# Hybrid streaming encoder layer: filler groups of 7, 8 and 6 per attention step, a twelfth Strassen pair, and the convolution ahead of the values copy

## The chip, the cores and the metric

The kernel runs on one core of one Trainium2 chip. The metric is the device time of one execution in microseconds (us), as the median of several runs. Before the change it is 1660.65 us (three runs, 1660.37 to 1661.24). Profiles come from one further execution each.

## The reference

One layer, 1024 prompt tokens and 8 x 16 sample tokens, 1152 tokens in all, width 1024, float32.

```
xn = rmsnorm(x)
[h | B | C | q | k | v | g_conv | g_attn] = xn @ w_in
u  = C * h
y_c = B * causal_conv3(u)                      # 3 taps, depthwise
y_a = sliding_window_attention(q, k, v, sinks) # 16 heads, 4 kv heads, window 128, chunks of 64
x = x + (sigmoid(g_conv) * y_c + sigmoid(g_attn) * y_a) @ w_out
x = x + (silu(rmsnorm(x) @ w_gate) * (rmsnorm(x) @ w_up)) @ w_down
```

It also returns the last rows of the convolution input and the new keys and values.

## The kernel before

**Precision.** Each large product is made of three matmuls in the fast float32 format: weights and activations are split into a high part (ACT copies it out) and a low part (POOL subtracts), and high x high, high x low and low x high are added up in PSUM.

**Stages, in order of time.** Norm and transposes; values, keys and queries; an attention stage; the late pairs; the output projection; the feed-forward part in two passes. The change touches the attention stage, the late pairs and what lies between them.

**Tiles.** The columns of w_in for h, C, B, g_conv and g_attn (kinds 0 to 4) fall into four blocks i of 256 columns, each of two halves jj of 128. A tile (i, jj, kind) is one half: 128 columns against 1152 tokens. It has three parts g of 384 tokens, each of 8 groups (one per 128 rows of the contraction), each group three matmuls of 384 columns (L2209). So a tile is 24 groups or 72 matmuls. `TILES` lists the tiles made this way: all five kinds of block 0, and kinds 0 to 3 of block 1, 18 tiles.

**Late pairs.** `LATE` lists the other (i, kind), 11 of them: both halves at once, as a product of 2 x 2 blocks by Strassen's scheme with 7 block products (L2269) of 24 matmuls with 288 columns. DVE adds and subtracts blocks of weights for it (`late_weight_sums`), ACT makes the high parts, POOL the low parts, and the sums of activations t1 to t4 are prepared by POOL (`t1_part`, `t2_part`), DVE (`t_op`, `t_low`) and ACT during and behind the attention stage.

**Attention.** There are 16 steps (block of heads i, 128 queries t) of three units u: two of four heads, and one of the sample tokens. Unit z = 24 i + 3 t + u, from 0 to 47. A unit goes through
- TensorE `s1`, its scores (L2141 to L2163);
- DVE `softmax_bias`: the maxima (L1442) and two small biases (L1444, L1447);
- ACT `exps`: exponentials (L1037, L1040);
- DVE `denominator` (L1454, L1457), then ACT's scaling (L1044);
- TensorE `s2`: transposes of the probabilities (L2174);
- DVE `out_transposed`: the values copy (L1430), which takes them out of PSUM;
- TensorE `s3`: probabilities times values (L2192, L2197), then ACT `out_attention`.

TensorE's queue is written out by hand so that fillers, the groups of `TILES` in order, hide these steps: in the stretch of unit z come `s1(z)`, `MIDDLE` = 4 fillers, `s2(z - 1)` (and in every third unit `s0`, a transpose of cached keys for the next step, whose result DVE copies out in `after_s0`, L1422), 4 more fillers, `s3(z - 1)`. `PER_SLOT` is 8, so a part of a tile is just one such stretch, and its last group is the last filler. Of 432 groups 384 lie in the stretches; the last two tiles follow behind them.

DVE's queue in the stretch of unit z: `softmax_bias(z)`, `out_transposed(z - 1)`, `after_s0` if u is 2, `denominator(z)`, then for parts that ended in z - 1 the convolution `conv` (kind 1; L1485 multiplies, L1487 twice multiplies and adds) or a gate (kinds 3 and 4), then for parts that end in z the product that takes them out of PSUM (kinds 1 and 2). `units_of(z)` gives the parts that end in z, `end_slot` where a part ends.

POOL's queue in a step: the low parts of a weight slab (`split_lo_quarters`, L665, four pieces), when the tile two before has ended, placed ahead of the staging if that is the step's first stretch and behind it otherwise; the staging of the next step's queries, keys and values (`stage`: L738, L742, L748, L754, L760, L769); in block 1 part sums for t1. In the last step the part sums for t2 (L820, L822) stand there. SP loads slabs and late weights, ACT splits high parts and evacuates kinds 0, 3 and 4.

Behind the stretches DVE's order is again by hand: a convolution, `t_op`, `t_low`, the products of the last two tiles and `late_weight_sums(0)`. The last tile's second and third parts swap banks (`LAST_BANKS`), and the first late product waits for the bank of the second part (`bank_free[2]`), the second product for the other two.

Of the kernel before, what the change touches and what calls it, by code (L numbers as in the profile page):

```python
# [28 lines left out]
ALU = mybir.AluOpType  # L29
# [34 lines left out]
        [(1, jj, kind) for jj in range(2) for kind in range(4)]  # L64
# [8 lines left out]
PER_SLOT = 8  # L73
MIDDLE = 4


def end_slot(n, g):

    return (24 * n + 8 * g + 7) // PER_SLOT
# [12 lines left out]
INSIDE = 2 * SLOTS * PER_SLOT // 24  # L92
# [106 lines left out]
class Slab:  # L199


    def __init__(self, first, per=0, i=0):
        self.n = first + per * i
        self.slot = first % 2
        self.turn = first // 2 + (per // 2) * i
        self.split = self.slot if isinstance(first, int) and first < OUT_SLAB else 1 - self.slot


LATE = [(1, 4)] + [(i, kind) for i in (2, 3) for kind in range(5)]
# [25 lines left out]
def build(nc, io):  # L235
    ctx = ExitStack()
    with ctx:
# [247 lines left out]
        def late_view(n, part):  # L485
            return ring_l[:, (n + 1) % LRING, part, :].rearrange("p (k c) -> p k c", k=4)
# [423 lines left out]
        def _(act):  # L910
# [185 lines left out]
            def late_slot_hi(n):  # L1096

                v, prod = n // 7, LATE_ORDER[n % 7]
                if n >= LRING:
                    act.wait_ge(l_used, n - LRING + 1)  # L1100
                else:
                    act.wait_ge(gemm_ready, 3 * (LATE_FEAT - 1 + (n + 1) % LRING // 2))
# [9 lines left out]
            unit(16, 0)  # L1112
            act.wait_ge(small_out, 32)
            act.activation(t1_hi[:, :, :], t1_f[:, :, :], ACT.Copy).then_inc(t_hi, 1)
            unit(16, 1)
            unit(16, 2)
            late_slot_hi(0)
            unit(17, 0)
            unit(17, 1)
            late_slot_hi(1)  # L1120
            unit(17, 2)
# [6 lines left out]
            def late_pair(v):  # L1128
# [16 lines left out]
                if v == 0:  # L1145
                    act.wait_ge(sg_used, 18)
                else:
                    act.wait_ge(lu2_done, v)
# [201 lines left out]
        def _(dve):  # L1350
# [119 lines left out]
            def conv(i, jj, g):  # L1470
# [5 lines left out]
                for k in range(3):  # L1476
# [12 lines left out]
                if g == 2:  # L1489
# [73 lines left out]
            for i in range(2):  # L1563
                for t in range(STEPS):
                    for u in range(3):
# [6 lines left out]
                        else:  # L1572
                            bi, bz = divmod(z - 1, SLOTS)
# [6 lines left out]
                        for n, g in units_of(z - 1):  # L1580
                            if TILES[n][2] == 1:
                                conv(*TILES[n][0:2], g)
                            if TILES[n][2] >= 3:
                                unit(n, g)
# [4 lines left out]
            conv(1, 1, 2)  # L1589
            dve.wait_ge(t_part, T2_PARTS)  # L1590
            dve.wait_ge(s3_done, 2 * SLOTS)
            t_op(t4_f[:, :, :], x_quad(0, 1, 0).bitcast(F32), t2_f[:, :, :], ALU.subtract)
            t_op(t3_f[:, :, :], t2_f[:, :, :], x_quad(0, 0, 0).bitcast(F32), ALU.subtract)
            t_low(1, t2_lo[:, :, :], t2_f[:, :, :], t2_hi[:, :, :])
            unit(16, 0)
            unit(16, 1)
# [3 lines left out]
            unit(16, 2)  # L1600
# [3 lines left out]
            unit(17, 0)  # L1604
            t_op(t4_f[:, :, :], t4_f[:, :, :], x_quad(1, 1, 0).bitcast(F32), ALU.add)
            unit(17, 1)
            unit(17, 2)
# [32 lines left out]
            def late_pair(v):  # L1640
# [39 lines left out]
                if kind == 3:  # L1680
# [4 lines left out]
                if v == 0:  # L1685
                    dve.wait_ge(sg_used, 18)
# [328 lines left out]
        def _(pe):  # L2015
# [200 lines left out]
            for i in range(2):  # L2216
                for t in range(STEPS):
                    for u in range(3):
# [22 lines left out]
            for k, group in enumerate(groups[2 * SLOTS * PER_SLOT:]):  # L2241
# [82 lines left out]
            def row_units(slot, s, act_slot):  # L2324
                for t in range(NT):
# [7 lines left out]
                    row_unit(3 + t % DU, ws[1 - slot], act_slot, t)  # L2333
# [28 lines left out]
            for n, (c, hf, t) in enumerate(LAST_ROWS):  # L2362
# [6 lines left out]
                row_unit(4 + n % 4, third if c == 2 else ws[1 - hf], c % 2, t)  # L2369
# [142 lines left out]
```

## Time and profile before

| what | us |
|---|---|
| median of 3 runs | 1660.65 (1660.37 to 1661.24) |
| the profiled execution | 1661.15 |
| its span | 1659.3 |
| TensorE busy | 1641.2 (99%) |
| DVE busy | 1041.4 (63%) |
| POOL busy | 972.5 (59%) |
| ACT busy | 726.4 (44%) |

The span runs from the first to the last instruction of the profiled execution; its own time is 1.85 us longer. Matmuls are pipelined, so a matmul's shown duration is longer than the distance from its start to the next one's, and a busy TensorE is one with no gap, not one at its peak. An idle time in brackets behind a row is that of its engine just ahead of the row, with what ended it; "issue" means that the profile names no releaser.

### The profile page before, as it was taken

The numbers are of one execution on the slowest core, as the hardware profiler recorded it, in microseconds if no ns is written. First come the engines' busy times: TensorE is split into PE (matmuls) and PEld (weight loads), VectorE is DVE, ScalarE is ACT, GpSimd is POOL, SyncE is SP. The second block draws the span as 40 slices with busy tenths as digits, with TensorE's granted clock in tenths as the row PEclk, the third lists the DMA queues.
The fourth block names the chain that finished last, engine by engine and source line by source line (L and its number), as shares of the span: only waits on it lengthen the run. The fifth ranks groups of instructions, "written<-read, shape, count | busy, mean of one in ns | idle before, by whom it ended". The sixth has DMA issues, their size and how long they took to land.

```text
span 1659.3 us, 28301 instructions
## 1 busy us (share of the span) xinstructions
PE 1641.2 (99%) x10775; PEld 1535.3 (93%) x10775; DVE 1041.4 (63%) x1602; ACT 726.4 (44%) x1635; POOL 972.5 (59%) x873
## 2 busy tenths in 40 slices
PE   7999999999999999999999999999999999999999
PEld 7999889998899999999889899999989999999998
DVE  6466664655659664475676767667687555555555
ACT  6333566666664313223155544544444433333331
POOL 3544533445554544443359978878878666666662
PEclk9999999999999999999999999999999999999999
DMA  5211111111110111114121333333233222222222
GB/s 180 49 39 38 48 33 33 33 33 33 41 38 13 52 52 52 52 45 159 53 90 51 105 113 95 98 113 102 91 130 104 84 77 89 77 80 86 87 79 76
DMA packets 124834, 120.44 MB, mean 73 GB/s; under 512 B 24218, under 2 KB 106430, under 8 KB 124704
## 3 DMA queue, kind: packets, MB, share of 16 engines
q1 hardware_dynamic: 119136, 115.89, 22.3%
q10 hardware_dynamic: 4896, 2.36, 0.5%
q8 instruction: 84, 1.38, 0.3%
q0 software_dynamic: 672, 0.43, 0.1%
q14 instruction: 46, 0.38, 0.1%
HBM read 113.34 MB, written 5.32 MB: 72 GB/s over the span
## 4 chain that ended last, share of the span: by engine, by line
PE 64%; DVE 2%; POOL 1%; issue 0%; ACT 0%; DVEq 0%; ACTq 0%
PE banks L2381 29%; PE banks L2442 15%; PE banks L2269 14%; PE banks L2319 5%; PE banks L2209 1%; PE banks L2464 1%; POOL ring_a L863 1%; PE banks L2358 0%; DVE act L1613 0%; DVE w_sums L1804 0%; DVE O L1659 0%; POOL ring_o L863 0%; DVE gate L1939 0%; DVE xc_full L1826 0%; POOL w_lo L658 0%
## 5 line engine op out<-in xcount | busy, mean ns | idle before, releaser
L2381 PE MATMUL banks<-xc_hi,ring_a 128*128 128x256 f32 (+1 forms) x1200 | 248.2, 296 | 0.6 <-POOL ring_a L863 0.6
L863 POOL TENSOR_TENSOR ring_a<-raw_f,ring_a 128x512 fp32r<-128x512 f32 x133 | 191.2, 1450 | 19.4 <-ACT ring_a L1232 18.4
L2381 PEld LDWEIGHTS banks<-xc_hi,ring_a 128*128 128x128 f32 x1200 | 196.6, 190 | 1.4 <-issue 1.0
L2381 PE MATMUL banks<-xc_lo,ring_a 128*128 128x256 f32 (+1 forms) x600 | 177.7, 296 | 0.0
L2209 PE MATMUL banks<-x_hi,w_hi 128*128 128x384 f32 x432 | 154.0, 356 | 0.3 <-DVE branch L1519 0.3
L1964 DVE TENSOR_TENSOR X<-banks,X 128x512 f32<-128x512 f32 x190 | 123.2, 683 | 36.4 <-PE banks L2442 36.2
L2209 PE MATMUL banks<-x_hi,w_lo 128*128 128x384 f32 x432 | 145.2, 336 | 0.0
L2209 PE MATMUL banks<-x_lo,w_hi 128*128 128x384 f32 x432 | 145.1, 336 | 0.0
L2269 PE MATMUL banks<-x_hi,late_ring 128*128 128x288 f32 x704 | 143.6, 295 | 0.0
L665 POOL TENSOR_TENSOR w_lo<-w_raw,w_hi 128x256 fp32r<-128x256 f32 x72 | 52.1, 756 | 147.2 <-ACT w_hi L916 147.2
L2381 PE MATMUL banks<-xc_hi,ring_o 128*128 128x256 f32 (+1 forms) x640 | 134.7, 296 | 0.0
L2442 PE MATMUL banks<-ring_a,h_act 128*128 128x512 f32 x570 | 133.3, 391 | 1.0 <-DVE X L1964 0.6
L2442 PEld LDWEIGHTS banks<-ring_a,h_act 128*128 128x128 f32 x570 | 105.9, 188 | 24.7 <-DVE X L1964 2.3
L863 POOL TENSOR_TENSOR ring_a<-w_sums,ring_a 128x512 fp32r<-128x512 f32 x60 | 85.2, 1420 | 73.8 <-ACT ring_a L1232 73.8
L2381 PEld LDWEIGHTS banks<-xc_lo,ring_a 128*128 128x128 f32 x600 | 113.8, 190 | 0.4
L2269 PEld LDWEIGHTS banks<-x_hi,late_ring 128*128 128x128 f32 x704 | 113.9, 188 | 0.0
L1232 ACT ACTIVATE ring_a<-raw_f 128x512 fp32r<-128x512 f32 x133 | 81.3, 624 | 73.3 <-PE banks L2442 54.3
L2269 PE MATMUL banks<-t_hi,late_ring 128*128 128x288 f32 x528 | 108.5, 295 | 0.0
L1393 DVE RECIPROCAL branch<-branch 128x384 f32<-128x384 f32 x30 | 76.6, 2552 | 48.5 <-ACT branch L986 48.5
L2381 PEld LDWEIGHTS banks<-xc_hi,ring_o 128*128 128x128 f32 x640 | 105.7, 190 | 0.2
L2269 PE MATMUL banks<-x_lo,late_ring 128*128 128x288 f32 x352 | 103.6, 294 | 0.0
L848 POOL TENSOR_TENSOR late_ring<-late_raw,late_ring 128x512 fp32r<-128x512 f32 x44 | 66.9, 1526 | 60.5 <-ACT late_ring L1107 60.5
(330 smaller groups left out, 4610.2 us busy)
## 6 DMA issues: line engine op xcount, KB each, us to landing
raw_f<-in_w_gate SPq DMA_DIRECT2D x88, 256.0 KB, 3.0
raw_f<-in_w_up SPq DMA_DIRECT2D x88, 256.0 KB, 3.1
raw_f<-in_w_down SPq DMA_DIRECT2D x88, 256.0 KB, 2.8
w_raw<-in_w_in SPq DMA_DIRECT2D x60, 256.0 KB, 3.4
late_raw<-in_w_in SPq DMA_DIRECT2D x44, 256.0 KB, 3.0
X<-in_x_prompt SPq DMA_DIRECT2D x16, 512.0 KB, 7.3
w_raw<-in_w_out SPq DMA_DIRECT2D x16, 256.0 KB, 3.0
out_y_prompt<-X SPq DMA_DIRECT2D x16, 256.0 KB, 2.0
```

What stands on the lines that cost most here:

```text
L665: ins = gp.tensor_tensor(ws[slab.split][1][:, part], raw[slab.slot][:, part], ws[slab.split][0][:, part].bitcast(F32), ALU.subtract)
L848: gp.tensor_tensor(late_view(n, 1), late_source(prod), late_view(n, 0).bitcast(F32), ALU.subtract)\
L863: gp.tensor_tensor(slot_view(n, 1), slot_source(n), slot_view(n, 0).bitcast(F32), ALU.subtract).then_inc(f_lo, 1)
L1232: act.activation(slot_view(n, 0), slot_source(n), ACT.Copy).then_inc(f_hi, 1)
L1393: dve.reciprocal(kr[:, bank[0], :], kr[:, bank[0], :]).then_inc(h_rs, 1)
L1964: dve.tensor_tensor(x, banks[:, row_bank(n), :], x, ALU.add).then_inc(y_free, 1)
L2209: mm = pe.matmul(banks[:, bank, 0:G], ws[n % 2][w][:, kt * P:(kt + 1) * P], xs[x][:, kt, g * G:(g + 1) * G], start=(kt == 0 and z == 0), s ...
L2269: mm = pe.matmul(banks[:, 2 * BANK_OF_PROD[prod] + u, 0:LN], late_view(n, w)[:, k, :], late_x(prod, x, u, k), start=(starts and k == 0 and ...
L2319: mm = pe.matmul(banks[:, bank, :], acts[act_slot][:, k, x, t * P:(t + 1) * P], split[w][:, k * 512:(k + 1) * 512], start=(k == 0 and n == ...
L2381: mm = pe.matmul(banks[:, bank, 0:nb], ring(n)[:, w, k * P:(k + 1) * P], xc[x][:, X_OF_PROD[j], k, 0:nb], start=(start and k == 0 and z == 0),
L2442: mm = pe.matmul(banks[:, row_bank(n), :], rows, ring(SLOT0[r] + 2 * hf + k)[:, w, :], start=(k == 0 and o == 0), stop=(k == 1 and o == 2))
L2464: mm = pe.matmul(banks[:, row_bank(n), :], rows, ring(SLOT0[r] + 2 * hf + k)[:, w, :], start=(c == NCH - 2 and k == 0 and o == 0), stop=(c ...
```

## The change

Two tiles, kind 3 of block 1, leave `TILES` (16 tiles left) and (1, 3) joins `LATE` (12 pairs). The fillers in the stretches are no longer 8 each but 7, 8 and 6 for the three units of a step, with 4, 5 and 3 of them ahead of `s2`. A part of a tile now ends anywhere in a stretch. DVE runs the convolution between `softmax_bias` and `out_transposed`, save for the third tap of a tile's last part, which stays behind `denominator`. Behind the stretches DVE's list is ordered anew; it has all three convolutions of tile (1, 1, 1). The late ring's slots are numbered so that the first two lie where the last tile but one had its weights. The first late pair's waits are those of a pair of kind 3.

```
-        [(1, jj, kind) for jj in range(2) for kind in range(4)]
+        [(1, jj, kind) for jj in range(2) for kind in range(3)]
...
-PER_SLOT = 8
-MIDDLE = 4
+GROUPS = (7, 8, 6)
+AHEAD = (4, 5, 3)
+FIRST_GROUP = [sum(GROUPS) * (z // 3) + sum(GROUPS[:z % 3]) for z in range(2 * SLOTS + 1)]
 def end_slot(n, g):
-    return (24 * n + 8 * g + 7) // PER_SLOT
+    last = 24 * n + 8 * g + 7
+    return sum(last >= first for first in FIRST_GROUP) - 1
...
-LATE = [(1, 4)] + [(i, kind) for i in (2, 3) for kind in range(5)]
+LATE = [(1, 3), (1, 4)] + [(i, kind) for i in (2, 3) for kind in range(5)]
...
-            return ring_l[:, (n + 1) % LRING, part, :].rearrange("p (k c) -> p k c", k=4)
+            return ring_l[:, n % LRING, part, :].rearrange("p (k c) -> p k c", k=4)
...
@@ DVE, in the stretch of unit z
                         else:
+                            for n, g in units_of(z - 1):
+                                if TILES[n][2] == 1:
+                                    conv(*TILES[n][0:2], g, range(3) if g < 2 else range(2))
                             bi, bz = divmod(z - 1, SLOTS)
                             out_transposed(bi, *divmod(bz, 3))
...
                         for n, g in units_of(z - 1):
-                            if TILES[n][2] == 1:
-                                conv(*TILES[n][0:2], g)
+                            if TILES[n][2] == 1 and g == 2:
+                                conv(*TILES[n][0:2], g, (2,))
                             if TILES[n][2] >= 3:
                                 unit(n, g)
...
@@ DVE, behind the stretches
             out_transposed(1, STEPS - 1, 2)
-            conv(1, 1, 2)
             dve.wait_ge(t_part, T2_PARTS)
             dve.wait_ge(s3_done, 2 * SLOTS)
             t_op(t4_f[:, :, :], x_quad(0, 1, 0).bitcast(F32), t2_f[:, :, :], ALU.subtract)
+            unit(14, 0)
+            conv(1, 1, 0)
+            t_low(1, t2_lo[:, :, :], t2_f[:, :, :], t2_hi[:, :, :])
+            unit(14, 1)
+            conv(1, 1, 1)
             t_op(t3_f[:, :, :], t2_f[:, :, :], x_quad(0, 0, 0).bitcast(F32), ALU.subtract)
-            t_low(1, t2_lo[:, :, :], t2_f[:, :, :], t2_hi[:, :, :])
-            unit(16, 0)
-            unit(16, 1)
+            unit(14, 2)
             dve.wait_ge(t_step, 2)
             dve.wait_ge(t_lo, 1)
             t_low(2, t1_lo[:, :, :], t1_f[:, :, :], t1_hi[:, :, :])
-            unit(16, 2)
-            t_op(t3_f[:, :, :], t3_f[:, :, :], x_quad(1, 0, 0).bitcast(F32), ALU.subtract, 2)
+            conv(1, 1, 2)
+            unit(15, 0)
             dve.wait_ge(t_lo, 2)
             late_weight_sums(0)
-            unit(17, 0)
+            unit(15, 1)
+            t_op(t3_f[:, :, :], t3_f[:, :, :], x_quad(1, 0, 0).bitcast(F32), ALU.subtract, 2)
+            unit(15, 2)
             t_op(t4_f[:, :, :], t4_f[:, :, :], x_quad(1, 1, 0).bitcast(F32), ALU.add)
-            unit(17, 1)
-            unit(17, 2)
...
@@ TensorE, in the stretch of unit z
-                        for k, group in enumerate(groups[z * PER_SLOT:(z + 1) * PER_SLOT]):
+                        for k, group in enumerate(groups[FIRST_GROUP[z]:FIRST_GROUP[z + 1]]):
...
-                            if k == MIDDLE:
+                            if k == AHEAD[u]:
```

## Rows read from the trace of the kernel before

**Rows 1.** The page, busy time of the engines: us, share of the span, instructions.

```profile
PE 1641.2 (99%) x10775; PEld 1535.3 (93%) x10775; DVE 1041.4 (63%) x1602; ACT 726.4 (44%) x1635; POOL 972.5 (59%) x873
```

**Rows 2.** The chain that ended last: start us, us, what; its late pairs.

```profile
535.76 235.34 PE banks L2269 x1776
```

**Rows 3.** TensorE in order of time, one attention step: start, us, line, operation.

```profile
388.51 0.28 PE L2141 MATMUL banks<-mask,halves 64*128 64x256 bf16 x2
...
393.27 0.33 PE L2209 MATMUL banks<-x_hi,w_lo 128*128 128x384 f32 x1
...
393.79 0.33 PE L2209 MATMUL banks<-x_hi,w_lo 128*128 128x384 f32 x1
393.96 0.38 PE L2197 MATMUL banks<-probsT,cache_v_rows 128*128 128x128 f32 x2
...
394.50 0.28 PE L2141 MATMUL banks<-mask,halves 64*128 64x256 bf16 x2
...
400.68 1.08 PE L2192 MATMUL banks<-probsT,v_stage 128*64 128x256 f32 x8
401.69 0.23 PE L2160 MATMUL banks<-window,halves 128*128 128x128 bf16 x1
...
407.56 1.08 PE L2192 MATMUL banks<-probsT,v_stage 128*64 128x256 f32 x8
408.57 0.28 PE L2141 MATMUL banks<-mask,halves 64*128 64x256 bf16 x2
```

**Rows 4.** DVE in order of time, the same step.

```profile
392.05 0.42 DVE L1430 COPY probsT<-banks 128x256 f32<-128x256 f32 x1 [0.37 <-PE banks L2174]
...
397.02 0.16 DVE L1447 TENSOR_TENSOR soft<-soft,sinkb 128x4 f32<-128x4 f32 x1
398.69 1.23 DVE L1430 COPY probsT<-banks 128x1024 f32<-128x1024 f32 x1 [1.51 <-PE banks L2174]
...
403.11 0.16 DVE L1447 TENSOR_TENSOR soft<-soft,sinkS 128x1 f32<-128x1 f32 x1
405.44 1.23 DVE L1430 COPY probsT<-banks 128x1024 f32<-128x1024 f32 x1 [2.17 <-PE banks L2174]
406.58 0.34 DVE L1422 TENSOR_SCALAR cache_kT<-banks,qnw 128x128 f32<-128x128 f32 x1
```

**Rows 5.** TensorE in order of time, the first two units: where it waited.

```profile
192.75 0.40 PE L2144 MATMUL banks<-mask,halves 64*128 64x256 bf16 x4 [0.32 <-ACT soft L1040]
...
199.94 1.08 PE L2192 MATMUL banks<-probsT,v_stage 128*64 128x256 f32 x8 [0.82 <-issue]
```

**Rows 6.** DVE in order of time, the first unit's values copy.

```profile
198.63 1.21 DVE L1430 COPY probsT<-banks 128x1024 f32<-128x1024 f32 x1
```

**Rows 7.** DVE in order of time, convolutions alone and beside POOL.

```profile
306.62 0.40 DVE L1485 TENSOR_SCALAR branch<-u,cwT 128x384 f32<-128x384 f32 x1
...
307.06 1.27 DVE L1487 SCALAR_TENSOR_TENSOR branch<-u,cwT,branch 128x384 f32<-128x384 f32 x2
...
502.55 3.36 DVE L1487 SCALAR_TENSOR_TENSOR branch<-u,cwT,branch 128x384 f32<-128x384 f32 x2
```

**Rows 8.** POOL in order of time, the step of rows 3.

```profile
390.92 2.82 POOL L665 TENSOR_TENSOR w_lo<-w_raw,w_hi 128x256 fp32r<-128x256 f32 x4 [8.31 <-ACT w_hi L916]
...
397.11 0.73 POOL L754 TENSOR_TENSOR k_lo<-k_full,k_hi 128x256 fp32r<-128x256 f32 x1
397.80 1.43 POOL L760 TENSOR_TENSOR q_lo<-O,q_hi 128x256 fp32r<-128x256 f32 x2
```

**Rows 9.** POOL in order of time, part sums beside the convolution at 502.55.

```profile
499.51 5.99 POOL L822 TENSOR_TENSOR t_full<-t_full,x_lo 128x576 f32<-128x576 f32 x4
```

**Rows 10.** TensorE in order of time, its waits from unit 47 to the late pairs.

```profile
508.33 1.08 PE L2192 MATMUL banks<-probsT,v_stage 128*64 128x256 f32 x8 [0.57 <-issue]
...
523.04 0.41 PE L2209 MATMUL banks<-x_hi,w_hi 128*128 128x384 f32 x1 [0.30 <-DVE branch L1519]
```

**Rows 11.** Busy by window, the two last tiles: window, length, PE, PEld, DVE, ACT, POOL.

```profile
509.30:535.60 26.30, 26.00 (x153) 25.67 (x152) 25.89 (x28) 8.69 (x14) 6.67 (x5) 1.00 0.07 21
```

More of the change, by code:

```diff
@@ L89, in slab_after @@
     return [n + 2 for n in range(len(TILES) - 2) if end_slot(n, 2) + 1 == z and z <= 2 * SLOTS]
-INSIDE = 2 * SLOTS * PER_SLOT // 24
 PASSES = ((0, 0), (0, 1), (1, 0))
@@ L205, in __init__ @@
         self.turn = first // 2 + (per // 2) * i
-        self.split = self.slot if isinstance(first, int) and first < OUT_SLAB else 1 - self.slot
-LATE = [(1, 4)] + [(i, kind) for i in (2, 3) for kind in range(5)]
+        self.split = self.slot
+LATE = [(1, 3), (1, 4)] + [(i, kind) for i in (2, 3) for kind in range(5)]
 GATED = [sum(kind >= 3 for _, kind in LATE[:v]) for v in range(len(LATE))]
@@ L1101, in late_slot_hi @@
                 else:
-                    act.wait_ge(gemm_ready, 3 * (LATE_FEAT - 1 + (n + 1) % LRING // 2))
+                    act.wait_ge(gemm_ready, 3 * (LATE_FEAT - 1 + n // 2))
                 if prod in (A11_PROD, A12_PROD, A22_PROD):
@@ L1145, in late_pair @@
                 if v == 0:
-                    act.wait_ge(sg_used, 18)
+                    act.wait_ge(sg_used, 12)
                 else:
@@ L1468, in sample_cols, with conv @@
                 return a[:, SEQ:TOK].rearrange("p (b c) -> p b c", b=DEC_B)
-            def conv(i, jj, g):
+            def conv(i, jj, g, steps=range(3)):
                 lo, hi = u_parts(g)
@@ L1475, in conv @@
                 dve.wait_ge(bank_free[LAST_BANKS[g] if n == len(TILES) - 1 else g], PAIR_FEAT + n + 1)
-                for k in range(3):
+                for k in steps:
                     w = cwT[:, k, bass.ds(2 * i + jj, 1)]
@@ L1488, in conv @@
                     ins.then_inc(conv_step, 1)
-                if g == 2:
+                if g == 2 and 2 in steps:
                     j = bass.ds(2 * i + jj, 1)
@@ L1592, in _ @@
             t_op(t4_f[:, :, :], x_quad(0, 1, 0).bitcast(F32), t2_f[:, :, :], ALU.subtract)
+            unit(14, 0)
+            conv(1, 1, 0)
+            t_low(1, t2_lo[:, :, :], t2_f[:, :, :], t2_hi[:, :, :])
+            unit(14, 1)
+            conv(1, 1, 1)
             t_op(t3_f[:, :, :], t2_f[:, :, :], x_quad(0, 0, 0).bitcast(F32), ALU.subtract)
-            t_low(1, t2_lo[:, :, :], t2_f[:, :, :], t2_hi[:, :, :])
-            unit(16, 0)
-            unit(16, 1)
+            unit(14, 2)
             dve.wait_ge(t_step, 2)
@@ L1599, in _ @@
             t_low(2, t1_lo[:, :, :], t1_f[:, :, :], t1_hi[:, :, :])
-            unit(16, 2)
-            t_op(t3_f[:, :, :], t3_f[:, :, :], x_quad(1, 0, 0).bitcast(F32), ALU.subtract, 2)
+            conv(1, 1, 2)
+            unit(15, 0)
             dve.wait_ge(t_lo, 2)
             late_weight_sums(0)
-            unit(17, 0)
+            unit(15, 1)
+            t_op(t3_f[:, :, :], t3_f[:, :, :], x_quad(1, 0, 0).bitcast(F32), ALU.subtract, 2)
+            unit(15, 2)
             t_op(t4_f[:, :, :], t4_f[:, :, :], x_quad(1, 1, 0).bitcast(F32), ALU.add)
-            unit(17, 1)
-            unit(17, 2)
             dve.wait_ge(gemm_ready, 3 * LATE_FEAT)
@@ L1679, in late_pair @@
                     dve.wait_ge(conv_step, 36 + 6 * (i - 2) + 3)
-                if kind == 3:
+                if v == 0:
+                    for b in range(3):
+                        dve.wait_ge(bank_free[b], LATE_FEAT)
+                elif kind == 3:
                     dve.wait_ge(lc11_done, v)
@@ L1684, in late_pair @@
                     dve.wait_ge(l_gated, g0)
-                if v == 0:
-                    dve.wait_ge(sg_used, 18)
                 dve.wait_ge(l_used, late_done(v, S3_PROD))
@@ L2240, in _ @@
                             s3(*before, used)
-            for k, group in enumerate(groups[2 * SLOTS * PER_SLOT:]):
+            for k, group in enumerate(groups[FIRST_GROUP[2 * SLOTS]:]):
                 if k == 0:
@@ L2332, in row_units @@
                         pe.wait_ge({0: lc11_done, 1: lc21_done, 3: lc12_done}[t], len(LATE))
-                    row_unit(3 + t % DU, ws[1 - slot], act_slot, t)
+                    row_unit(3 + t % DU, ws[slot], act_slot, t)
             for c in range(3):
@@ L2368, in _ @@
                 pe.wait_ge(d_free, (43, 44, 45, 45)[n] if n < 4 else LAST_BASE + n - 3)
-                row_unit(4 + n % 4, third if c == 2 else ws[1 - hf], c % 2, t)
+                row_unit(4 + n % 4, third if c == 2 else ws[hf], c % 2, t)
                 if n == 12:
```

## The prediction

> **What bounds the kernel now.** I read the busy shares first: TensorE is busy 99% of the span [rows 1]. With one engine that full, a change can only move the time by giving TensorE fewer or shorter instructions, or by making it wait. Then the chain of waits: through the Strassen products of the late pairs it is TensorE alone, 1776 matmuls in 235.34 us, so 132.5 ns each [rows 2]. Then TensorE's order of time through one attention step [rows 3]: the scores of its three units start at 388.51, 394.50 and 401.69, the next step at 408.57. A step takes 20.06 us, its units 5.99, 7.19 and 6.88, and fillers run from end to end: three filler matmuls, one group, take 0.52 us (393.27 to 393.79). I write "slot" for the stretch of one unit, slots 0 to 47, and give times in a slot from its first scores matmul.
>
> Last, what TensorE would wait for next. At the end of each slot it multiplies the previous unit's probabilities by the values (L2192, L2197), which needs DVE's values copy (L1430), in third slots also the copy of the cached keys behind it (L1422). The copy starts when the transposes end. In a second slot it runs from 398.69 for 1.23, the product starts at 400.68: 0.76 to spare. In a third slot the keys copy ends at 406.92, the product starts at 407.56: 0.64 to spare. In a first slot it is 1.49 [rows 3, 4]. TensorE can start 0.10 behind such a copy: where it waited for one, the copy ended at 199.84 and the product began at 199.94 [rows 5, 6].
>
> **The change, part by part.**
>
> **Fewer fillers.** Three groups leave each of the 16 steps: 48 groups at 0.52. The first gives nothing. In slot 0 TensorE already waits for ACT's exponentials (idle 0.32), and in slot 1 for the values copy (idle 0.82) [rows 5]; that copy follows a chain on DVE which no filler sets, so both slots end when they did. 47 x 0.52 = 24.4 us off.
>
> **One more late pair.** 7 products x 24 matmuls = 168 x 132.5 ns = 22.3 us on [rows 2]. ACT, POOL and DVE take this pair like the eleven others, beside which TensorE never waited. The weights loaded are the same bytes. Both parts together: 2.1 us off.
>
> Here a rule speaks against the change. The rows price a matmul by its columns: 173 ns at 384 columns [rows 3], 132.5 ns at 288 [rows 2], so 168 of the short cost less than 144 of the long. The Trainium skill (TensorE: Matmul & The Clock Gate, Back-to-back issue gap) gives sustained spacings of 81 ns at 128 columns and 131 ns at 512. An estimate on a line between them, 114 and 102 ns, makes the late pair 17.1 us and the two tiles 16.5, so the sum would be 3.3 us worse than mine. I go by the rows, both taken in this kernel.
>
> **The places of the three transposes and values products.** Behind the transposes (AHEAD 4, 5, 3) every slot keeps three groups where it had four. The spare times above fall by 0.52: first slots 0.97, second 0.24, third 0.12. All are over 0.10, the last by a hair. I take no cost for slots without a convolution.
>
> **The convolution ahead of the values copy.** It is a multiply (0.40) and two multiply-adds (0.63 each) on DVE, 1.7 with the gaps [rows 7]. Behind the denominators it delayed no values copy; now it can. Three tiles of products h*C lie in the slots, and their nine parts run in slots 5, 6, 7; 19, 20, 21; 39, 40, 41 (a part's convolution runs in the slot after its last group; tiles of 24 groups against steps of 21 give the slots). The last part of each tile leaves its third tap behind the denominators, so it counts four short instructions.
>
> Third slots (5, 20, 41): DVE ends the maxima and biases at 1.58 (403.11 + 0.16), the convolution at 3.28, and the values copy starts at 3.75 - 0.52 = 3.23 [rows 4]. So near that I take no cost.
>
> Second slots (7, 19, 40): biases end at 2.68, the values copy is due at 4.19 + 0.52 = 4.71 [rows 4]. Alone the convolution would end at 4.38. But POOL stages the next step's queries and keys there, from 2.61 to 4.73 [rows 8]. DVE and POOL instructions on SBUF operands don't run together: against POOL's pieces of 1.50 us each multiply-add took 1.68 instead of 0.63 [rows 7, 9]. Here the pieces are 0.72, so my estimate is 0.87 for the multiply (it waits out the piece running until 3.34) and 1.1 per multiply-add: end at 5.7, values copy until 6.9, product at 7.0 in place of 6.18: 0.8 us. Four short instructions in slot 7: 1.0. Together 2.6.
>
> First slots (6, 21, 39): biases also at about 2.7, convolution 4.4, copy of one block (0.42 to 0.43) 4.8, product due at 5.45 - 0.52 = 4.93 [rows 3, 4]. Slot 6 fits. Slot 39 meets the end of a POOL part sum which now stands behind a slab split of slot 38: 0.3, my guess. Slot 21 meets the split of a weight slab, four pieces from 2.41 to 5.23 [rows 8]; each of the four instructions waits for one, they end near 6.0, the product starts near 6.5: 1.5.
>
> Sum 4.4 us on. Below it, the cost is 0 if POOL's pieces and the convolution miss each other; above, 8.8 if each instruction waits for twice as much. I take the middle, because these POOL pieces stand at fixed distances from the scores in every step, so the overlap is not a matter of luck.
>
> **The last slots.** In slot 47 TensorE idled 0.57 [rows 10] because DVE was late from a convolution stretched by POOL's part sums. No convolution is left there, but the small bias steps still meet those sums: 0.3 off (between 0 and 0.6).
>
> **Behind the slots.** DVE was busy 25.89 of the 26.30 us of the two last tiles [rows 11], TensorE waited once for it, 0.30 [rows 10]. DVE now has three convolutions there instead of one (3.4 more) but comes in without a backlog. It must release the bank of the last tile's second part before the late products start, and by the order in the code that falls about when TensorE arrives: 0.3 on, between -0.3 and 2. Queued behind that release are the release for the second product and the sums for the fourth, with about 1 us each to spare.
>
> Sum: -24.4 + 22.3 + 4.4 - 0.3 + 0.3 = 2.3 us on. The profiled execution took 1661.15 us (span 1659.3), 0.5 over the median of 1660.65. The same 2.3 on the median is 1662.9.
>
> **The rivals.**
>
> *The convolution hides.* If POOL's pieces miss it, 4.4 falls away: -2.1, or 1658.5 us. For it: alone it fits every slot but the third ones, by 0.05. Against it: the pieces in [rows 8] lie right across it. Chance 0.25. It is a gain, but inside the 0.2% (3.3 us) that a measurement of this kernel can tell from no change. For more than that, all waits of the old slots and tail would have to vanish too: 0.04 of this.
>
> *The short slots lose their margin (slower).* Place: second and third slots without convolution, some 26 of them. With 0.24 and 0.12 left against 0.10, it decides from 0.14 and 0.02 us of delay of the values copy. A wait of 0.15 in each adds 3.9 to the forecast: 1666.8 us. For it: the 0.02. Against it: no row shows DVE late for the transposes there. Chance 0.15.
>
> *The step doesn't shrink.* If the softmax chain sets the pace, TensorE stands still where fillers were and the late pair is paid in full: 1660.65 + 22.3 = 1683. Against it: every slot had at least 0.6 to spare [rows 3, 4]. Chance 0.01.
>
> *Matmuls cost by number, not by columns.* Then the late pair costs 24 matmuls more than the tiles, 24 x 132.5 ns = 3.2 in place of -2.7, and the time is 1668.8. The rows speak plainly against it; 0.01. The rule cited above points this way, and by the two spacings the trace does not agree.
>
> **How the numbers follow.** Forecast 0.58, convolution hides 0.25, margin 0.15, the rest 0.02. The forecast's own range is 1659.5 to 1666.5 from the bounds of its terms; about a quarter of it lies over 1664.0, the limit of slower. Slower: 0.58 x 0.25 + 0.15 + 0.02 = 0.31. Faster by over 0.2%: 0.04. No change: 0.65. The range 1658.2 to 1666.6 takes in the hidden case and most of the margin case.
>
> **What would show it.** The filler line L2209 with 1152 matmuls instead of 1296, L2269's successor with 2016 instead of 1848 at 132.5 ns. A step near 18.5 us between first-unit scores. New TensorE waits before the values product in slots 7, 19, 21 and 40 of 0.7 to 1.6 us, with multiply-adds of about 1.1 us there; none in 5, 6 and 20. If these slots show no wait, the contention step is wrong; if plain second and third slots show waits, the margin step is; if the time falls by more than 3 us, something in the old slots cost what I did not see.

## The result, and the profile after

The changed kernel takes **1663.1 us** (median of 20 runs, 1662.55 to 1663.9) against 1660.65 for the kernel before: a ratio of 1.0015, 95% interval 1.0008 to 1.0022. That is slower, by less than the 0.2% counted as no change here. The profiled execution took 1663.34 us, its span is 1661.6 us, 2.3 over the span before. In the page of the changed kernel, busy us and instructions by engine, to be read against [rows 1]:

```profile
span 1661.6 us, 28376 instructions
PE 1640.2 (99%) x10799; PEld 1534.2 (92%) x10799; DVE 1044.9 (63%) x1609; ACT 729.7 (44%) x1639; POOL 985.0 (59%) x872
```

TensorE is busy 1.0 us less than before and the span is 2.3 longer: the work became a little cheaper and TensorE waits 3.3 us more. Where, the stretches tell. First the kernel before: the attention stage (first scores to the last transposes), the two tiles behind it, and its first late pair. Columns: window, length, PE, PEld, DVE, ACT, POOL, granted clock, DMA share, GB/s.

```profile
186.47:509.35 322.88, 321.17 (x2310) 288.24 (x2309) 194.14 (x404) 209.54 (x711) 147.71 (x223) 1.00 0.12 34
509.35:535.60 26.25, 25.95 (x153) 25.66 (x152) 25.84 (x28) 8.69 (x14) 6.67 (x5) 1.00 0.07 21
535.60:557.86 22.26, 22.26 (x169) 22.26 (x169) 15.64 (x15) 11.13 (x15) 14.33 (x8) 1.00 0.16 48
```

The same of the changed kernel, the last line being its first late pair:

```profile
186.43:489.37 302.94, 297.54 (x2166) 264.71 (x2165) 185.81 (x393) 206.13 (x706) 143.79 (x215) 1.00 0.11 33
489.37:515.08 25.71, 25.71 (x153) 25.70 (x151) 22.73 (x31) 8.41 (x14) 9.48 (x6) 1.00 0.08 22
515.08:537.99 22.91, 22.76 (x170) 22.33 (x169) 20.38 (x15) 10.13 (x13) 18.06 (x8) 1.00 0.15 47
```

The attention stage is 19.94 us shorter, but TensorE's idle time in it (length less PE's busy time) went from 1.71 to 5.40. The two tiles are 0.54 shorter. There is one more late pair at 22.26, and the first one takes 0.65 more than that. Sum: -19.94 - 0.54 + 22.26 + 0.65 = +2.43, the 2.3 of the spans to within 0.15. In the chain that ended last, the late pairs read as 1872 matmuls at 132.7 ns, where [rows 2] has 132.5, behind a slow first pair:

```profile
518.54 6.60 PE banks L2276 x48
525.16 248.33 PE banks L2276 x1872
```

The new idle time is in TensorE's waits of the changed kernel (total us, times, longest). L2199 and L2204 are the values products, L2192 and L2197 of before:

```profile
PE banks L2199 <- issue: 2.5, 4, 0.8
PE banks L2204 <- issue: 1.4, 2, 1.1
PE banks L2151 <- ACT soft L1041: 0.8, 1, 0.8
PE banks L2199 <- DVE cache_kT L1423: 0.4, 1, 0.4
```

Of these, 0.82 of the first row (slot 1) and 0.32 of the third (slot 0) are old [rows 5]. Slot 0 waits 0.52 more, because it has a group less and ends no sooner; that part of the 3.69 us costs nothing by itself.

"issue" hides the releaser here. It is found by laying DVE beside TensorE. TensorE in order of time from slot 19 (a second slot, scores at 305.46) to slot 21:

```profile
305.46 0.28 PE L2148 MATMUL banks<-mask,halves 64*128 64x256 bf16 x2
312.29 1.08 PE L2199 MATMUL banks<-probsT,v_stage 128*64 128x256 f32 x8 [0.58 <-issue]
...
318.14 1.08 PE L2199 MATMUL banks<-probsT,v_stage 128*64 128x256 f32 x8
319.16 0.28 PE L2148 MATMUL banks<-mask,halves 64*128 64x256 bf16 x2
325.40 0.46 PE L2204 MATMUL banks<-probsT,cache_v_rows 128*128 128x128 f32 x2 [1.15 <-issue]
```

DVE in order of time in slot 19, with the keys copy of slot 20 and the two multiplies of slot 21:

```profile
306.50 1.23 DVE L1443 TENSOR_REDUCE soft<-banks 128x4 f32<-128x1024 f32 x1 [1.05 <-PE banks L2161]
...
308.06 0.97 DVE L1486 TENSOR_SCALAR branch<-u,cwT 128x384 f32<-128x384 f32 x1
309.07 1.98 DVE L1488 SCALAR_TENSOR_TENSOR branch<-u,cwT,branch 128x384 f32<-128x384 f32 x2
310.98 1.21 DVE L1431 COPY probsT<-banks 128x1024 f32<-128x1024 f32 x1
...
317.65 0.34 DVE L1423 TENSOR_SCALAR cache_kT<-banks,qnw 128x128 f32<-128x128 f32 x1
...
322.24 1.58 DVE L1486 TENSOR_SCALAR branch<-u,cwT 128x256 f32<-128x256 f32 x2
```

POOL in order of time, beside it and beside slot 21:

```profile
306.74 0.62 POOL L749 TENSOR_TENSOR k_hi<-kT,qnw 128x256 fp32r<-128x256 f32 x1
...
308.07 0.74 POOL L755 TENSOR_TENSOR k_lo<-k_full,k_hi 128x256 fp32r<-128x256 f32 x1
308.78 1.86 POOL L761 TENSOR_TENSOR q_lo<-O,q_hi 128x256 fp32r<-128x256 f32 x2
310.58 0.73 POOL L770 COPY v_stage<-V 128x256 f32<-128x256 f32 x1
...
321.55 2.87 POOL L666 TENSOR_TENSOR w_lo<-w_raw,w_hi 128x256 fp32r<-128x256 f32 x4 [10.24 <-ACT w_hi L917]
```

The convolution takes 2.99 us where it takes 1.7 alone [rows 7], DVE goes straight on to the values copy, and the product starts 0.10 behind that copy's end, TensorE having idled 0.58. In slot 21 the product waits 1.15 in the same way, behind a convolution that meets the slab split. POOL pays too: its two pieces take 0.93 each instead of 0.72 [rows 8]. The Trainium skill (SBUF — State Buffer, Who interferes with whom) says that a DVE instruction with two SBUF inputs contends with a GpSimd instruction that reads SBUF, and that one with at most one SBUF input, outside the modes that use both ports, does not, a reduction never. The trace agrees in direction: the multiply-add goes from 0.63 to 0.99, while the maxima (1.23) and the values copy (1.21), both read from PSUM with POOL at work beside them, stay as they were alone. The multiply goes from 0.40 to 0.97 although a single tensor is its input; no row tells in which mode it ran.

Against the plain length of their kind (5.47, 7.19, 5.84 us), the slots of the changed kernel are longer by

| slot | kind | us over plain | what is late |
|---|---|---|---|
| 7, 19, 40 | second | 0.54, 0.65, 0.64 | convolution beside POOL's staging |
| 21 | first | 1.39 | convolution beside a slab split |
| 39 | first | 0.46 | convolution behind a bias stretched by a part sum |
| 29 | third | 0.48 | the two small biases beside POOL |
| 36 | first | 0.32 | the same, by way of the exponentials |
| 14 third slots | third | 0.02 to 0.04 each, 0.5 together | copy of the cached keys |
| 5, 6, 20, 41 | first, third | none (third: as above) | |
| 0 and 1 | first, second | none: 14.49 together, as before | |

### The profile page after: what moved, and what is told of

It reads as the page before. It is cut to its first block, busy times and chain, and to the rows that moved or that the text cites. A ratio compares the mean times of both kernels' runs of the same rounds, so it can differ in the third digit from the quotient of the medians.

```text
span 1661.6 us, 28376 instructions
## 1 busy us (share of the span) xinstructions
PE 1640.2 (99%) x10799; PEld 1534.2 (92%) x10799; DVE 1044.9 (63%) x1609; ACT 729.7 (44%) x1639; POOL 985.0 (59%) x872
## 3 DMA queue, kind: packets, MB, share of 16 engines
q1 hardware_dynamic: 118112, 115.89, 22.3%
q8 instruction: 84, 1.38, 0.3%
## 4 chain that ended last, share of the span: by engine, by line
PE 94%; DVE 2%; POOL 1%; issue 1%; ACT 1%; DMA 0%; SPq 0%; DVEq 0%; ACTq 0%
PE banks L2388 28%; PE banks L2276 16%; PE banks L2449 15%; PE banks L2216 12%; PE banks L2035 7%; PE banks L2326 5%; PE banks L2199 2%; PE banks L2181 2%; PE banks L2058 2%; PE banks L2161 1%; PE banks L2071 1%; PE banks L2471 1%; POOL ring_a L864 1%; PE banks L2048 0%; PE banks L2170 0%
## 5 line engine op out<-in xcount | busy, mean ns | idle before, releaser
L2276 PE MATMUL banks<-x_hi,late_ring 128*128 128x288 f32 x768 | 156.8, 295 | 0.0
L2216 PE MATMUL banks<-x_hi,w_hi 128*128 128x384 f32 x384 | 137.9, 359 | 0.0
L2216 PE MATMUL banks<-x_hi,w_lo 128*128 128x384 f32 x384 | 129.1, 336 | 0.0
L2216 PE MATMUL banks<-x_lo,w_hi 128*128 128x384 f32 x384 | 129.0, 336 | 0.0
L2276 PEld LDWEIGHTS banks<-x_hi,late_ring 128*128 128x128 f32 x768 | 124.2, 188 | 0.3 <-DVE x_lo L1546 0.3
L2276 PE MATMUL banks<-t_hi,late_ring 128*128 128x288 f32 x576 | 118.5, 295 | 0.1
L2276 PE MATMUL banks<-x_lo,late_ring 128*128 128x288 f32 x384 | 113.1, 294 | 0.0
L849 POOL TENSOR_TENSOR late_ring<-late_raw,late_ring 128x512 fp32r<-128x512 f32 x48 | 75.2, 1573 | 62.0 <-ACT late_ring L1108 62.0
L849 POOL TENSOR_TENSOR late_ring<-late_sums,late_ring 128x512 fp32r<-128x512 f32 x36 | 53.5, 1489 | 85.0 <-ACT late_ring L1108 85.0
```

Of the source, the lines that this page charges most:

```text
L849: gp.tensor_tensor(late_view(n, 1), late_source(prod), late_view(n, 0).bitcast(F32), ALU.subtract)\
L2216: mm = pe.matmul(banks[:, bank, 0:G], ws[n % 2][w][:, kt * P:(kt + 1) * P], xs[x][:, kt, g * G:(g + 1) * G], start=(kt == 0 and z == 0), s ...
L2276: mm = pe.matmul(banks[:, 2 * BANK_OF_PROD[prod] + u, 0:LN], late_view(n, w)[:, k, :], late_x(prod, x, u, k), start=(starts and k == 0 and ...
```

## The experiments

**What does the convolution cost ahead of the copy, if POOL is kept away?** The changed kernel, with POOL's staging held in the three steps whose second slot has a convolution:

```
             if q >= 1:
                 gp.wait_ge(s1_done, 3 * (q - 1) + 2)
+                if q - 1 in (2, 6, 13):
+                    gp.wait_ge(pt_ready, 3 * (q - 1) + 1)
             gp.wait_ge(k_step, q + 1)
```

> The changed kernel; in the three steps whose second slot has a convolution, POOL's low parts of keys and queries wait until the values copy of that slot is done. Theory (DVE and POOL hold each other up): the convolutions of slots 7, 19 and 40 take 1.7 us in place of 2.9, the slots fall to 7.19, 1.8 us together, less up to 0.5 for what POOL now does later: 1661.3 to 1661.9 us. Rival (the convolution is too long for its place by itself): 1662.8 to 1663.4, slots 7, 19 and 40 as before.

Measured: **1660.76 us** (1660.42 to 1661.89), 2.3 below the changed kernel; to the kernel before 0.9999, interval 0.999 to 1.0008. DVE in slot 19, in order of time:

```profile
307.67 0.41 DVE L1488 TENSOR_SCALAR branch<-u,cwT 128x384 f32<-128x384 f32 x1
308.12 1.27 DVE L1490 SCALAR_TENSOR_TENSOR branch<-u,cwT,branch 128x384 f32<-128x384 f32 x2
309.77 1.23 DVE L1433 COPY probsT<-banks 128x1024 f32<-128x1024 f32 x1 [0.39 <-PE banks L2183]
```

The convolution is back at its length alone, DVE now waits 0.39 for the transposes, and slots 7, 19 and 40 are plain (7.19). So in those slots the whole cost was the meeting with POOL, not the new place. The stage is 1.81 shorter, the sum of the three slots; the profiled execution (1661.75, the second longest of the eleven) is 1.59 below that of the changed kernel. The median fell by 0.5 more than the stage, and by more than expected, which no row settles.

**Is the new place worth anything?** All convolutions put back behind the denominators, the rest of the change kept:

```
-                            for n, g in units_of(z - 1):
-                                if TILES[n][2] == 1:
-                                    conv(*TILES[n][0:2], g, range(3) if g < 2 else range(2))
...
-                            if TILES[n][2] == 1 and g == 2:
-                                conv(*TILES[n][0:2], g, (2,))
+                            if TILES[n][2] == 1:
+                                conv(*TILES[n][0:2], g)
```

> The changed kernel with all nine convolutions back behind the denominators; fillers, late pairs and everything else as changed. Theory (the convolution ahead of the values copy makes TensorE wait): slots 7, 19, 21, 39 and 40, which are 0.54, 0.65, 1.39, 0.46 and 0.64 us longer than plain ones (3.7 together), fall back to 7.19 and 5.47 us. New delays are possible where the four-part convolutions of slots 7 and 41 now end after the next scores: up to 0.4 in slot 8 and 1.6 in slot 42. So 1659.4 to 1661.5 us. Rival (behind the denominators the convolution holds up the next maxima by as much, which is why it was moved): 1662.5 us or more.

Measured: 1663.07 us, ratio 1.0016 (1.0007 to 1.0025), the same as the changed kernel. The waits moved: slots 7, 19, 21, 39 and 40 are plain, but the slot after a convolution is long, 8 by 0.56, 22 by 0.54, 42 by 2.25, because DVE comes to its maxima 2.3, 2.7 and 3.2 us late. DVE around slot 42 (scores at 449.45):

```profile
448.47 1.30 DVE L1486 TENSOR_SCALAR branch<-u,cwT 128x256 f32<-128x256 f32 x2
449.80 3.77 DVE L1488 SCALAR_TENSOR_TENSOR branch<-u,cwT,branch 128x256 f32<-128x256 f32 x4
...
453.64 1.22 DVE L1443 TENSOR_REDUCE soft<-banks 128x4 f32<-128x1024 f32 x1
```

The estimate in the expectation was too small for slot 42. The expected 1659.4 to 1661.5 us was missed, and the rival of the expectation came true: with short slots a convolution finds no place on DVE that is free by itself, 3.35 us of waits behind, 3.68 ahead. Slot 43 added 1.41 in this profile from another cause (the last section).

**The third slots' missing 0.03.** The same kernel with the transposes a group earlier in second and third slots:

```
-AHEAD = (4, 5, 3)
+AHEAD = (4, 4, 2)
```

> As e1_conv_behind, and the transposes one group earlier in second and third slots (4, 4, 2 groups ahead in place of 4, 5, 3). Theory (the 0.03 to 0.04 us that 14 third slots are longer than counted is the keys copy ending too near the values product): third slots at 5.84 instead of 5.88, 0.5 us; the denominators come 0.5 earlier, so what e1 has of new delays in slots 8 and 42 shrinks too: 0.5 to 1.5 us below e1. Rival (those 0.04 are the cost of issuing, not a wait): within 0.2 us of e1.

Measured: 1661.7 us, 1.4 below. The plain third slots take 5.83 to 5.84 instead of 5.87 to 5.88, 0.5 in all; slot 42 is 0.77 better, slot 2 0.26 worse. There the transpose of the cached keys starts at 202.90, 0.14 behind the last of ACT's rows that take the first unit's output out of PSUM; the probabilities, which the text of a later run blames, are scaled by 201.37, ahead of their transposes at 201.73.

**How near is the edge?** The changed kernel with the transposes one group later everywhere:

```
-AHEAD = (4, 5, 3)
+AHEAD = (5, 6, 4)
```

> The changed kernel with the transposes one group later in every slot (5, 6, 4 in place of 4, 5, 3). Theory (the spare time behind the copies is 0.97, 0.24 and 0.15, and 0.10 to 0.15 of it is the least there can be): second slots without convolution get 0.38 longer (13 of them), third slots 0.5 (16), first slots don't change: 13 us, so 1676 us. Rival (there is more slack than the profile shows, as in the queue of TensorE): under 1668 us.

Measured: 1675.23 us in a single execution, 1676 expected. The waits of this kernel name the late part:

```profile
PE banks L2199 <- DVE cache_kT L1423: 7.4, 15, 0.5
PE banks L2199 <- issue: 6.5, 17, 0.8
```

Third slots are longer by 0.54 to 0.56, second by 0.38 to 0.39, first ones not at all, save slot 42 by 0.54. Call the 0.10 us from a copy's end to the product's start the hand-over. With a margin m over it, a group of 0.52 should cost 0.52 - m: that gives 0.14 for second slots (predicted 0.24 - 0.10), and for third slots 0.52 on top of the 0.03 that they had already lost (predicted 0.12 - 0.10 to spare). The margins read in the trace of before were right to 0.06.

**Slots 21, 29, 36 and 39.** The changed kernel with the slab split ahead of slot 21's step held until the values copy, and the part sums of three steps held until the biases:

```
                     for n in slab_after(z):
+                        if z == 21:
+                            gp.wait_ge(pt_ready, z)
                         split_lo_quarters(Slab(PAIR_SLAB + n))
...
+                    if i == 1 and t in (1, 3, 4):
+                        gp.wait_ge(soft_done, 5 * {1: 29, 3: 36, 4: 39}[t] + 3)
                     if i == 1 and 1 <= t < 7:
```

> The changed kernel with GpSimd's work moved out of the way of VectorE in three places and nothing else: the weight split ahead of slot 21's step waits for slot 21's values copy, and the t1 sums that fell on slots 29, 36 and 39 wait for those slots' second bias. The convolution stays ahead of the values copy. Theory (what slows the convolution and the biases is GpSimd reading and writing SBUF at the same time): slot 21 goes back to its plain 5.47 us or to within 0.1 of it (it had 1.39 more), slots 29, 36 and 39 lose 0.48, 0.32 and 0.2 to 0.45 of what they had over plain; together 2.2 to 2.7 less, 1660.4 to 1660.9 us; slots 7, 19 and 40, where nothing is held, keep their 0.5 to 0.65 each. Rival (slots 21 and 39 are long because a convolution ahead of the copy is too long for a first slot with seven fillers, whatever GpSimd does): slot 21 keeps 1.0 or more of its extra and slot 39 its 0.46, and the time stays at 1662.0 to 1662.6. Second rival (GpSimd's held work comes late and meets another slot): the four slots are cured and others get longer, 1661.5 or more.

Measured: 1663.01 us over eleven executions, one of which took 5241.14 us, with no row to explain it; the other ten have a median of 1662.8. That is a gain of 0.3 us at most where 2.2 to 2.7 were expected, and the reason is in one slot. Slots 21, 29 and 36 are plain, 2.2 us less, as the theory says. Slot 39 went from 0.46 to 1.94 over. DVE and POOL there:

```profile
433.38 0.16 DVE L1452 TENSOR_TENSOR soft<-soft,sinkb 128x4 f32<-128x4 f32 x1
433.46 0.41 DVE L1490 TENSOR_SCALAR branch<-u,cwT 128x384 f32<-128x384 f32 x1
433.91 3.34 DVE L1492 SCALAR_TENSOR_TENSOR branch<-u,cwT,branch 128x384 f32<-128x384 f32 x2
```

```profile
433.62 3.21 POOL L810 TENSOR_TENSOR t_full<-t_full,x_lo 128x576 f32<-128x576 f32 x2 [2.48 <-DVE soft L1452]
```

The second bias releases the sums, and in a slot with a convolution the convolution stands right behind that bias: each multiply-add waits out one sum of 1.6 us (1.67 in place of 0.63). The stage is 0.70 shorter (1.39 + 0.48 + 0.32 - 1.48); the span is 0.3 shorter, as the stage began 0.35 later in this profile.

**All held together:** the holds of the first experiment and of the last one, and the transposes of the third slots a group earlier (`AHEAD = (4, 5, 2)`):

> The kernel with the staging held back in three steps (1660.76 us) plus the held split and sums, plus the transposes of the probabilities one filler group earlier in the third slots (AHEAD of 2 instead of 3 there), where the key copy had been 0.03 to 0.04 late in 14 slots. Theory: 2.2 to 2.7 for the held work and 0.3 to 0.5 for the third slots, less up to 0.3 in slot 2, where the scaled probabilities come late: 1657.8 to 1658.6 us, faster than the kernel before (1660.65) by 0.13 to 0.17 per cent. Rival (cured slots only hand the delay on): 1660 or more.

Measured: 1660.26 us (1659.82 to 1662.59), over the 1658.6 expected. Slots 7, 19, 40, 21, 29, 36 and all third slots but the first are plain; slot 2 has 0.31, and slot 39 keeps its 1.96, since its sums are still released ahead of the convolution. That slot alone is as large as the miss; the three longest executions are a matter of the last section.

**Are fillers free in slots 0 and 1?** Three groups more there, and six fillers instead of seven in slots 3, 9 and 12 (the "2+1" in the text is a slip for these):

```
-FIRST_GROUP = [sum(GROUPS) * (z // 3) + sum(GROUPS[:z % 3]) for z in range(2 * SLOTS + 1)]
+FIRST_GROUP = [sum(GROUPS) * (z // 3) + sum(GROUPS[:z % 3]) + (0, 2, 3, 3, 2, 2, 2, 2, 2, 2, 1, 1, 1, 0)[min(z, 13)]
+               for z in range(2 * SLOTS + 1)]
```

> The kernel of the run before it with two more filler groups in slot 0 and one more in slot 1, taken from slots 2+1, 9 and 12 (three first slots with six fillers: slots 3, 9 and 12). Slots 0 and 1 take 6.29 and 8.20 us, 0.8 and 1.0 over what their fillers need, because a chain other than the fillers ends them. Theory (fillers there are free): slots 0 and 1 grow by 0.2 at most together, slots 3, 9 and 12 lose 0.52 each: 1.2 to 1.6 less, 1656.4 to 1657.3 us. Rival (the fillers only push the chain back, since matrix products of the chain stand behind them in the same order): slots 0 and 1 grow by 1.0 or more, and the time stays within 0.5 of the run before it. Second rival (a first slot of six fillers is too short for the values copy and the exponentials): slots 3, 9, 12 lose less than 0.3 each.

Measured: 1659.39 us (1658.71 to 1660.09). Slots 0 and 1 take 6.41 and 8.07, 14.48 together as before, so three groups (1.56 us) cost nothing there; slots 3, 9 and 12 lose 0.53 each. The time fell by only 0.87, and 1656.4 to 1657.3 us, set before the run ahead of it was known, was missed: that run had not come down to 1658.6, and in this profile slot 40 took 1.54 more (the last section).

**The sums of slot 39 behind the copy.** The sums of slot 39's step wait for the values copy, which is behind the convolution, and slot 2 keeps its three fillers ahead of the transposes:

```
-                    if i == 1 and t in (1, 3, 4):
-                        gp.wait_ge(soft_done, 5 * {1: 29, 3: 36, 4: 39}[t] + 3)
+                    if i == 1 and t in (1, 3):
+                        gp.wait_ge(soft_done, 5 * {1: 29, 3: 36}[t] + 3)
+                    if i == 1 and t == 4:
+                        gp.wait_ge(pt_ready, 39)
...
-                            if k == AHEAD[u]:
+                            if k == AHEAD[u] + (z == 2):
```

> The kernel with filler groups moved into slots 0 and 1 (1659.39 us) with two repairs: the t1 sums of slot 39's step wait for slot 39's values copy, which comes behind the convolution, and not for its second bias, which comes ahead of it (there the two sums started together with the convolution, each multiply-add took 1.67 us, and the slot got 1.94 over plain); and slot 2 keeps its three fillers ahead of the transposes. Theory (a convolution ahead of the copy costs a first slot nothing but what GpSimd's SBUF work beside it adds): slot 39 returns to 5.47 us or to within 0.1 of it, slot 2 loses 0.3, and with the 1.7-us idle time of slot 39 gone the stretch at half clock behind it (1.54 us in slot 40 of the profile of the run before) is gone from all executions: 1656.7 to 1657.5 us in median, and no execution above 1658.2. Rival (slot 39 is too long with the convolution ahead, alone too): the slot keeps 0.4 or more and the median is 1657.6 or more.

Measured: **1657.0 us** (1656.6 to 1657.88), ratio to the kernel before 0.9979, interval 0.997 to 0.9988: below the kernel before, though not clearly by more than the 0.2% counted as no change, and 6.1 us below the changed kernel. Its busy times by window, the attention stage:

```profile
186.06:482.50 296.44, 296.09 (x2166) 263.35 (x2165) 179.31 (x393) 205.86 (x706) 142.41 (x215) 1.00 0.12 34
```

TensorE idles 0.35 us in the stage, against 5.40 in the changed kernel and 1.71 before. DVE and POOL in slot 39:

```profile
429.45 0.41 DVE L1495 TENSOR_SCALAR branch<-u,cwT 128x384 f32<-128x384 f32 x1
429.89 1.27 DVE L1497 SCALAR_TENSOR_TENSOR branch<-u,cwT,branch 128x384 f32<-128x384 f32 x2
431.08 0.42 DVE L1440 COPY probsT<-banks 128x256 f32<-128x256 f32 x1
```

```profile
431.58 2.81 POOL L813 TENSOR_TENSOR t_full<-t_full,x_lo 128x576 f32<-128x576 f32 x2 [4.42 <-DVE probsT L1440]
```

With POOL away, the convolution ahead of the copy costs this first slot nothing. The one cost left is 0.16 in slot 40, where the staging, pushed back by the held sums, meets the convolution. Of the 3.65 us to the kernel before, 1.6 belong to the moved groups. They were not tried on the kernel before, whose slots 0 and 1 wait too [rows 5]; nor were the holds, but in its stage TensorE waits nowhere outside slots 0, 1 and 47 (0.32 + 0.82 + 0.57 are the whole 1.71). The other 2 or so are what the change is worth with POOL ordered around it.

## Why the prediction was right

Predicted 1662.9, measured 1663.1. The mechanism held in the main: short slots, a late pair by its columns, the convolution against POOL. That it came out to 0.2 us is luck, since the errors of its terms, -1.2 and +1.3, cancel.

| step | predicted | found | from |
|---|---|---|---|
| fewer fillers | -24.4 | -24.4 | stage -19.94, less all rows below that lie in it |
| convolution ahead of the copy | +4.4 | +3.68 | slots 7, 19, 21, 39, 40 |
| plain slots' margin | 0 | +0.5 | 14 third slots at 0.02 to 0.04 |
| small biases beside POOL | not seen | +0.80 | slots 29 and 36 |
| slot 47 | -0.3 | -0.51 | its wait, 0.57 to 0.06 |
| behind the slots | +0.3 | +0.1 | -0.54 in the two tiles, +0.65 in the first late pair |
| late pair | +22.3 | +22.26 | each of the other eleven |
| sum | +2.3 | +2.43 | spans: 2.3 |

**Fewer fillers.** The -24.4 found is what the other rows leave, but the plain slots say the same: 16 first slots shorter by 0.52 and 16 third by 1.04, less the 0.52 of slot 0. That the first step gives nothing is confirmed by slots 0 and 1, 14.49 in both kernels with one group less, and again with three groups more.

**The late pair.** By the columns: 22.26 against 22.3. The spacings of the Trainium skill that the prediction weighed (TensorE: Matmul & The Clock Gate, Back-to-back issue gap) would have made the sum 3.3 us worse; the trace after does not agree with them, nor with the rival of cost by number. The filler line has its 1152 matmuls, the late line 2016, and a step without waits is 18.50 us.

**The convolution.** The mechanism and the places were right: waits in 7, 19, 21, 39 and 40, none in 6, and in 5, 20 and 41 no more than in any third slot. Holding POOL back removed it whole (1.81 us in three slots, 1.39 in slot 21). The sizes: the multiply took 0.97 (estimate 0.87), the multiply-adds 0.99 (1.1), so the second slots lost 0.65 instead of 0.8, less than the 0.7 named as the least wait to look for; slot 7's fourth instruction did not add the 0.2 I gave it (0.54 instead of 1.0). The sums of 1.50 that the prediction reads in [rows 9] are a mean of four, with those that were stretched themselves; alone such a sum takes 1.4. Slot 21 was 1.39 for 1.5, slot 39 0.46 for a guess of 0.3. The rival that it hides is refuted as the kernel stands, and true once POOL is ordered around it.

**The margins.** "I take no cost for slots without a convolution" failed by a hair: the keys copy ends 0.15 ahead of the product (317.65 + 0.34 to 318.14) instead of the 0.12 read, and TensorE starts 0.02 to 0.04 later than its fillers would let it. The step that failed is the 0.10 taken as the hand-over of every copy; behind the keys copy it is 0.15. The slower rival thus came true in place and sign, at about an eighth of its price (0.5 for 3.9), and not in second slots.

**What was not in the prediction.** The small biases (four columns each, one in a third slot; 0.16 us) read two SBUF operands too. In slot 29, beside two part sums that come behind a slab split, they take 1.16 and 1.34:

```profile
371.72 1.16 DVE L1445 SCALAR_TENSOR_TENSOR soft<-sinkS,soft 128x1 f32<-128x1 f32 x1
372.92 1.34 DVE L1448 TENSOR_TENSOR soft<-soft,sinkS 128x1 f32<-128x1 f32 x1
374.18 1.21 DVE L1431 COPY probsT<-banks 128x1024 f32<-128x1024 f32 x1
```

I named them for slot 47 alone. The same meetings cost nothing in longer slots; with three fillers less per step they do, 0.80 in two slots, and holding the sums removed both.

**Slot 47.** Its wait fell from 0.57 to 0.06, by 0.51; I had left 0.2 for small biases that meet part sums, and there they were not late for anything.

**Behind the slots.** Right near zero, wrong inside: DVE was not late in the two tiles (22.73 busy of 25.71, TensorE without a wait), but the first late pair was, by 0.65, in the starts of its second and fourth products, at 518.54 and 525.16 in the chain above. DVE there:

```profile
517.90 0.54 DVE L1520 TENSOR_TENSOR branch<-banks,branch 128x384 f32<-128x384 f32 x1
521.47 3.64 DVE L1546 TENSOR_TENSOR x_lo<-t_full,x_hi 128x2304 fp32r<-128x2304 f32 x1
```

The second product starts 0.10 behind the end of the first row, which takes the last part of the last tile out of its bank; the fourth starts 0.05 behind the second row, which makes its low part. Each row stands behind a sum of DVE (`t_op`) of 3.18 us. The prediction names both places, with "about 1 us each to spare"; that spare was not there. No run changed their order.

**The range.** The bounds that the terms name add up to 1657.65 and 1669.35, not to the forecast's own 1659.5 to 1666.5, and the chance of slower rests on the narrower pair.

## What to carry to other kernels

A slot that is shortened by a known amount turns every meeting of DVE and GpSimd that had been hidden into a wait, so list all DVE instructions on SBUF operands in it, the four-element ones with two inputs and the multiplies too, and not only those that the change moves. Before moving work on DVE, ask which GpSimd work lies beside its new place: here a wait on GpSimd, which has 40% of the span free, took 1.81 us off three slots, while two different places of the convolution on DVE cost much the same (3.35 and 3.68). Release held work behind the last DVE instruction that it could meet, not behind the first one: the wrong semaphore cost 1.5 us in one slot.

## What the runs showed of the hardware

**Instructions that meet take turns, whatever their size.** A multiply-add of 0.63 us took 0.99 beside pieces that take 0.72 alone and 1.67 beside sums that take 1.4 alone; a four-element bias of 0.16 took up to 1.38 (slot 36). The price goes by the length of the GpSimd instruction. The Trainium skill (SBUF — State Buffer, SBUF: two separate sides) says that of a DVE instruction with two SBUF inputs and a GpSimd instruction that reads SBUF, whichever starts first holds the shared ports for its whole instruction; these numbers agree with it.

**Half clock behind a wait.** In the run with groups moved into slots 0 and 1, slot 40 was 1.54 us too long in the profile, with no wait in it. TensorE had idled 1.71 us at the end of slot 39:

```profile
433.64 0.46 PE L2211 MATMUL banks<-probsT,cache_v_rows 128*128 128x128 f32 x2 [1.71 <-issue]
```

Its windows behind that (the third number from the right is the granted clock):

```profile
434.60:435.60 1.00, 1.00 (x13) 0.78 (x9) 0.00 (x0) 1.00 (x4) 1.00 (x4) 0.54 0.23 69
435.60:436.60 1.00, 1.00 (x5) 1.00 (x4) 0.95 (x1) 0.61 (x4) 1.00 (x2) 0.50 0.06 13
436.60:437.60 1.00, 1.00 (x4) 1.00 (x4) 0.93 (x4) 0.49 (x3) 0.11 (x1) 0.50 0.22 66
437.60:438.60 1.00, 1.00 (x6) 1.00 (x6) 0.93 (x3) 1.00 (x6) 0.00 (x0) 0.76 0.00 0
```

The clock is at its lower level, 1.2 GHz, for some 3 us. Four of this run's eleven executions show a mean clock of 0.999. In the run before it the same wait of 1.72 us was followed by full clock:

```profile
435.05 0.46 PE L2210 MATMUL banks<-probsT,cache_v_rows 128*128 128x128 f32 x2 [1.72 <-issue]
434.00:438.00 4.00, 2.95 (x26) 2.72 (x27) 2.92 (x7) 2.37 (x8) 2.33 (x6) 1.00 0.08 20
```

but there three of eleven executions, at 1662.25 to 1662.59, have a mean clock of 0.999 and stand 2 us over the other eight. The run with the slab split and the sums held had full clock behind a wait of 1.70 too. With the convolutions behind, waits of 1.14 and 0.80 were followed by 0.50 from 457.2 to 460.4, which is the 1.41 of slot 43; five of its eleven executions show 0.999 and lie 1.0 to 2.2 over the others. So a wait of 1.7 us cost sometimes about twice its length (1.71 + 1.54 in this profile); what decides it in an execution, no row shows. The last run, without such a wait, had 1.000 in all eleven executions, and they lie within 1.3 us.
